# Scores of blocks 0 and 1, and of blocks 2 and 3, each in one run of 64-row products

## The reference

```
h = RMSNorm(x);  z = h @ w_in            # q, k, v of 8 heads
q, k = rope(q), rope(k)                  # two maps per head, 64 wide each
s = q @ k.T * 64**-0.5                   # per head, per map, causal
p = softmax(where(mask, s, -1e30))
a = p[map 0] - lam * p[map 1]
o = RMSNorm(a @ v) * (1 - lam_init)
```

## Time and profile before

| what | value |
|---|---|
| median of 3 runs | 1675.25 us (1673.26 to 1676.34) |
| profiled execution | span 1673.1 us, no other time is listed for it; granted TensorE clock 0.998 |
| PE busy | 1654.3 us, 99% of the span, 12028 products |
| DVE busy | 1199.4 us, 72% |
| ACT busy | 745.6 us, 45% |
| POOL busy | 139.5 us, 8% |
| DMA | 194.73 MB, mean 116 GB/s |

### The profile page before, as it was taken

One profiled execution on the slowest core, in us unless ns is written; L12 is line 12 of the kernel. 1 busy time (PEld: TensorE's weight loads), 2 busy tenths in 40 slices (PEclk: granted clock), 3 DMA queues, 4 the chain that ended last, 5 costly groups with the idle time before them and its releaser, 6 DMA issues.

```text
span 1673.1 us, 30382 instructions
## 1 busy us (share of the span) xinstructions
PE 1654.3 (99%) x12028; PEld 1598.3 (96%) x12028; DVE 1199.4 (72%) x1989; ACT 745.6 (45%) x1524; POOL 139.5 (8%) x244
## 2 busy tenths in 40 slices
PE   8999999999999999999999999999999999999997
PEld 7899999999988999999999999999999999999997
DVE  6777777777777779776444468767666786868685
ACT  5455555555555321465312344343433543544352
POOL 3222312322210000000000000000000000000001
PEclk9999999999999999999999999999999999999999
DMA  6202202202204547575221222444444833443323
GB/s 198 64 1 76 70 14 71 77 17 61 71 1 151 180 127 240 181 261 188 89 64 58 82 89 95 140 140 140 140 140 140 308 104 128 152 149 131 107 83 127
DMA packets 153071, 194.73 MB, mean 116 GB/s; under 512 B 7642, under 2 KB 121370, under 8 KB 150874
## 3 DMA queue, kind: packets, MB, share of 16 engines
q1 hardware_dynamic: 138352, 160.59, 30.0%
q10 hardware_dynamic: 14578, 32.20, 5.3%
HBM read 148.86 MB, written 44.13 MB: 115 GB/s over the span
## 4 chain that ended last, share of the span: by engine, by line
PE 95%; DVE 3%; ACT 1%; issue 1%; DMA 0%; SPq 0%; DVEq 0%; POOL 0%; ACTq 0%; POOLq 0%
PE ps L1218 36%; PE ps L948 26%; PE ps L853 16%; PE ps L912 4%; PE ps L879 3%; PE ps L902 2%; PE ps L1271 1%; PE ps L1328 1%; PE ps L883 1%; PE ps L821 1%; PE ps L846 0%; PE ps L845 0%; PE ps L863 0%; PE ps L862 0%; PE ps L1120 0%
## 5 line engine op out<-in xcount | busy, mean ns | idle before, releaser
L853 PE MATMUL ps<-w_hi,h_hi 128*128 128x384 f32 x520 | 182.0, 350 | 0.3 <-DVE w_lo L1871 0.3
L853 PE MATMUL ps<-w_hi,h_lo 128*128 128x384 f32 x520 | 176.2, 339 | 0.0
L853 PE MATMUL ps<-w_lo,h_hi 128*128 128x384 f32 x520 | 175.4, 337 | 0.0
L1218 PE MATMUL ps<-d_hi,m_hi 128*128 128x258 f32 x784 | 158.7, 284 | 0.5 <-DVE x L2537 0.4
L1218 PE MATMUL ps<-d_lo,m_hi 128*128 128x258 f32 x784 | 159.2, 284 | 0.0
L1218 PE MATMUL ps<-d_hi,m_lo 128*128 128x258 f32 x784 | 158.2, 283 | 0.0
L1408 ACT ACTIVATE prob<-ps,nbias 128x256 f32<-128x256 f32 (+7 forms) x128 | 95.0, 742 | 78.7 <-DVE nbias L1934 76.4
L1669 ACT ACTIVATE m_hi<-m_pair 128x512 fp32r<-128x512 f32 (+1 forms) x128 | 76.9, 601 | 104.1 <-PE ps L1218 90.1
L1218 PEld LDWEIGHTS ps<-d_hi,m_hi 128*128 128x128 f32 x784 | 121.6, 190 | 1.0 <-DVE x L2537 0.6
L1218 PEld LDWEIGHTS ps<-d_hi,m_lo 128*128 128x128 f32 x784 | 122.3, 190 | 0.0
L1218 PEld LDWEIGHTS ps<-d_lo,m_hi 128*128 128x128 f32 x784 | 121.9, 190 | 0.0
(11 more groups left out here) (308 smaller groups left out, 4339.4 us busy)
## 6 DMA issues: line engine op xcount, KB each, us to landing
ff_combination_scratch<-ff_st SPq DMA_DIRECT2D x14, 1806.0 KB, 6.9
d_raw<-ff_combination_scratch ACTq DMA_DIRECT2D x21, 1032.0 KB, 7.3
w_raw<-in_w_in SPq DMA_DIRECT2D x41, 512.0 KB, 5.4
kv_pages<-in_cache_k SPq DMA_DIRECT2D x32, 512.0 KB, 5.3
kv_pages<-in_cache_v SPq DMA_DIRECT2D x32, 512.0 KB, 4.5
m_pair<-in_w_up SPq DMA_DIRECT2D x16, 1024.0 KB, 9.7
m_pair<-in_w_down SPq DMA_DIRECT2D x24, 512.0 KB, 5.2
out<-kv_st SPq DMA_DIRECT2D x16, 512.0 KB
```

What stands on the lines that cost most here:

```text
L853: mm = pe.matmul(bank[0:n, 0:3 * P], a[:, kt, toks(t)], w[:, :, kt, :], start=(kt == 0 and m == 0), stop=(kt == KT - 1 and m == 2))
L1218: mm = pe.matmul(acc[:, c], w[:, kt], a[:, kt % kts, c * CW:(c + 1) * CW], start=(opens and kt == 0 and m == 0), stop=(kt == n - 1 and m = ...
```

## The change

Blocks 0 and 1: one function, `first_scores`, does the products of both and then the four masks. Block 1's scores now begin at column 128, beside those of block 0, in the same banks. Its first product no longer clears the accumulation state of the bank, since the first product of block 0 has done so. VectorE's maxima of both blocks wait for all four masks.

Blocks 2 and 3, in heads 0 to 6: `middle_scores` does the same in step 2, behind the first half of the projection of tile 2. Block 3's scores begin at column 512 (banks 3 and 5), and wait until the projection of tile 1 has been read out of bank 3. In step 3 there are no scores; the transposes of block 2's weights stand ahead of the first half of the projection of tile 3 instead of behind it. In the last head blocks 2 and 3 stay apart.

```diff
         def first_col(h, i):
-            return 512 if h == HEADS - 1 and i == 2 else 0
+            return {1: P, (2 if h == HEADS - 1 else 3): 512}.get(i, 0)
...
-            def scores(h, par, i):
...
+            def score_passes(h, par, i):
                 diag, o = i // 4, first_col(h, i)
...
-                                      k[part, par, 1, 512 * b:512 * b + n], start=(m == 0),
-                                      stop=(m == 2))
+                                      k[part, par, 1, 512 * b:512 * b + n], start=(m == 0 and i != 1),
+                                      stop=(m == 2), skip_group_check=(i < 2))
...
+            def first_scores(h, par):
+
+                pe.wait_ge(s_qklo, 8 * h + 2)
+                need(pe, s_exp, 16 * h)
+                score_passes(h, par, 0)
+                score_passes(h, par, 1)
+                causal_mask(h, 0)
+                causal_mask(h, 1)
+
+            def middle_scores(h, par):
+
+                pe.wait_ge(s_qklo, 8 * h + NTT)
+                pe.wait_ge(s_exp, 16 * h + 4)
+                score_passes(h, par, 2)
+                pe.wait_ge(s_zfree, z_before(h + 1, 2) + 1)
+                score_passes(h, par, 3)
+                causal_mask(h, 2)
+                causal_mask(h, 3)
...
                 for s in range(NTT + 1):
-                    if s < NTT:
+                    if s == 0:
+                        first_scores(h, par)
+                    elif 4 <= s < NTT:
                         scores(h, par, s)
+                    if s == 2:
+                        project(h + 1, s, 0)
+                        middle_scores(h, par)
                     if 2 <= s < NTT:
                         values(h, par, s - 2)
                     elif s == 0 and normed:
                         values(h - 1, 1 - par, NTT - 1)
-                    project(h + 1, s, 0)
+                    if s == 3:
+                        weight_transposes(h, s - 1, 0, True)
+                    if s != 2:
+                        project(h + 1, s, 0)
...
-                    if s >= 1:
+                    if s >= 1 and s != 3:
                         weight_transposes(h, s - 1, 0, True)
...
             def maximum(h, i, c):
                 n = (i + 1) * P
                 k = 16 * h + 2 * i + c + 1
-                dve.wait_ge(s_s, k)
+                dve.wait_ge(s_s, 16 * h + 4 if i < 2 else k)
```

More of the change, by code:

```diff
@@ L879, in scores, with causal_mask @@
                             pe.matmul(bank_s[:, c, o + 512 * b:o + 512 * b + n], q[part, par, 0, i * P:(i + 1) * P],
-                                      k[part, par, 1, 512 * b:512 * b + n], start=(m == 0),
-                                      stop=(m == 2))
+                                      k[part, par, 1, 512 * b:512 * b + n], start=(m == 0 and i != 1),
+                                      stop=(m == 2), skip_group_check=(i < 2))
+            def causal_mask(h, i):
+                o = first_col(h, i)
                 for c in range(2):
@@ L884, in scores @@
                               skip_group_check=True).then_inc(s_s, 1)
+            def first_scores(h, par):
[13 more added lines that the diff above has]
+                causal_mask(h, 3)
+            def scores(h, par, i):
+                if h < HEADS - 1:
+                    pe.wait_ge(s_exp, 16 * h + 2 * i)
+                    if i == 4:
+                        pe.wait_ge(s_zfree, z_before(h + 1, NTT))
+                else:
+                    if i == 2:
+                        pe.wait_ge(s_qklo, 8 * h + NTT)
+                        pe.wait_ge(s_zs, HEADS - 1)
+                    pe.wait_ge(s_exp, 16 * h + 2 * (i - 1 if i <= 3 else i))
+                score_passes(h, par, i)
+                causal_mask(h, i)
             def weight_transposes(h, i, r, proj):
@@ L1045, in last_head @@
                 for s in range(NTT + 1):
-                    if s < NTT:
+                    if s == 0:
+                        first_scores(h, par)
+                    elif 2 <= s < NTT:
                         scores(h, par, s)
```

## The result

The changed kernel takes 1680.34 us (median of 6, 1678.30 to 1681.04) against 1674.65 (median of 6, 1673.26 to 1676.34): ratio 1.0032, 95% interval 1.0021 to 1.0042, slower by 5.7 us. Forecast were 1679.4 and +4.2. The profiled execution has a span of 1678.9 and a time of 1680.87; against the 1673.1 before, the span is 5.8 longer.

What follows compares the result with a forecast made beforehand. TensorE was taken as the bound, with 95% of the span. Heads 1 to 6 at +0.52 us each (3.1), head 0 +0.72 and last head +0.4 gave +4.2 on the 1675.25 median: 1679.4 us, range 1673.5 to 1683.

Steps and rivals of the forecast that it cites:

- Part 4: Heads 0 to 6: TensorE waits 1.40 us up to projection 3 for block 2's softmax and the copy; net 1.07 later.
- T: TensorE's start on projection 2; forecast from it: maximum at 3.90 us, copy's end at 8.83, projection 3 at 8.98.
- Part 1: Scores of blocks 0 and 1 in one run: saves 0.35 us per head, 2.8 us in eight heads.
- Part 2: Scores of blocks 2 and 3 in one run, heads 0 to 6: saves 0.33 us per head, 2.3 in seven.
- Part 3: Heads 1 to 6, projection behind block 0's scores: later arrival hides the wait for weights, 0.2 us each, 1.2 in all.
- low-weights wait: Projection behind block 0's scores, heads 1 to 6: waits 1.9 us over six load-queue waits for VectorE's low half; forecast gone.
- Part 5: Last head: VectorE's first maximum waits for all four masks, so the head ends about 0.4 us later.
- Head 0: First head, which has no wait for the weights to hide: forecast 0.72 us longer.
- The first: Rival: block 2's softmax or rotation runs beside TensorE, no wait comes, the merge pays: 1669.4 us, faster; 12%.
- The second, a smaller wait: Rival: the wait is smaller or more is hidden elsewhere; net +0.2 us per head, 1676.8 us; 20%.
- The third, a second wait: Rival: transposes of previous head's output wait for ScalarE to empty their bank; six heads lose 0.4 to 0.8, 1683; 8%.

Runs made afterwards that it cites:

- e2_middle_only: Changed kernel with blocks 0 and 1 apart as before, so only blocks 2 and 3 share a run: 1682.10 us, 1.0043 against the kernel before.
- e3_masks_apart: Changed kernel with block 2's masks right behind block 2's products, ahead of block 3's: 1674.91 us, 1.0000 against the kernel before.
- e1_first_only: Changed kernel with blocks 2 and 3 as before, so only blocks 0 and 1 share a run: 1673.65 us, 0.9992 against the kernel before.
- e6_first_not_last: Kernel before with blocks 0 and 1 in one run in heads 0 to 6, the last head unchanged: 1672.28 us, 0.9985 against the kernel before.
- e4_rotation_first: Changed kernel, VectorE rotating tile 2 before block 2's weights, block 2's transposes behind projection 3's first half: 1679.71 us, 1.0026 against the kernel before.

## Why the prediction was right

The direction, the place and the mechanism were right, and the size nearly: +4.2 forecast, +4.6 in the heads, +5.7 by the runs (3.5 to 7.0 by the interval). How close the time itself came (1679.4 against 1680.34) is in part luck. It was added to the 1675.25 of three runs, and six give 1674.65. The 1.04 us by which head 0 begins later have no term in the sum. And in the heads larger errors cancel: heads 1 to 5 are 0.4 over the forecast in all, head 0 is 0.16 over, head 6 is 0.28 under.

- *Part 4, the wait.* Right in each step. The points from T on are met within 0.03 us, and e2_middle_only gives its net price alone: 1.1 per head (1.07). What made it countable is that the order on VectorE is fixed: 4.93 us from maximum to copy before the change, 4.94 after (261.60 to 266.54).
- *Part 1.* The merge of blocks 0 and 1 pays 0.30, not 0.35. After the change, from 245.69 + 0.11 to the second product of values less its 0.12 are 1.27 us for the two blocks. Before, block 0 alone took 0.75, read in the same way from the first two rows below, and block 1 alone 0.82. The mis-sized term is the price of block 1 inside the run (0.35 + 0.12): its first pair takes 0.17 and not 0.12. That is 0.05 in each of heads 0 to 6, 0.35 in all.

```profile
242.65 0.27 PE L863 MATMUL ps<-ident,kv_st 128*128 128x128 f32 x1
...
243.63 0.28 PE L912 MATMUL ps<-v_hl,aT_lo 128*128 128x256 f32 x1
...
245.39 0.34 PE L853 MATMUL ps<-w_hi,h_hi 128*128 128x384 f32 x1
```

- *Part 2.* By TensorE's rows the merge of 2 and 3 is worth 0.33 as forecast: block 2's values start their second product at 261.74 in the changed kernel, 1.83 after the end of the half projection at 259.79, against 0.99 and 1.18 for the two runs apart (block 3's read in the same way). But it could never be cashed while projection 3 waits (e3_masks_apart): it only made the wait longer. I had booked it as income and the wait in full, which gives the same sum.
- *Part 3.* The low-weights wait is gone where blocks 0 and 1 are merged and there where they are not (e1_first_only, e2_middle_only). Its worth was met too: before, 24 products took 4.41 (245.39 to 249.80); after, 36 take 6.31, so 24 take 4.21: 0.20, as forecast. In the changed kernel it pays, since the wait behind blocks 2 and 3 counts from TensorE's own mask. In head 6 this wait was 0.37 longer than in the others, and the forecast treats all six alike: that is why head 6 came out lower than forecast.
- *Part 5.* Right: 0.42 measured, 0.4 forecast, and e6_first_not_last takes it back.
- *Head 0* was 0.88 longer and not 0.72. Part 1's 0.05 is in it (e1_first_only: -0.30). The rest lies behind T: to the turned q and k of tile 3 it takes 13.20 us after the change, as counted (8.98 + 4.20), but took 12.03 before, where the counted terms give 12.11. So TensorE's own work was counted 0.08 too long for this head; which term is at fault is not shown.
- *Rivals.* The first was out by 0.6 us of chain, as argued. The second, a smaller wait, is out as well: 9.0 less TensorE's own 7.58 is the 1.4 forecast. The third, a second wait, did not occur in the changed kernel, but its margin of 0.4 was real: e4_rotation_first ran into it.

In the changed kernel, too, pairs in the same two row groups start 0.12 apart with a load each (246.45 to 246.57). The Trainium skill's rule that a load overlaps running products only where the row group differs ("TensorE: Matmul & The Clock Gate", Part 3, The mechanism) is not borne out by these rows. The same section of the Trainium skill also says that a load which targets the background weight buffer is pulled ahead of running products. With that its words and the rows agree, and the prediction, which took only the narrower sentence, was wrong to find the Trainium skill at odds with the trace. No run here shows which buffer a load went to.

## What to carry to other kernels

A saving on the engine that is busy all the time is worth what it says only up to the next signal that this engine waits for. Before work is moved, write down for each consumer behind it how long the other engines' chain is, from the instruction whose end starts it, in the kernel's own rows. As long as the order on those other engines stays, the chain's length stays (4.93 and 4.94 here), and what changes is its cover. A new order on them can change it: in e4_rotation_first the copy ended 3.96 us after the maximum's start, and what was moved behind it took 0.39 longer than in its old place. Where work is put in one run to save a switch, let what others wait for come first, or put independent work behind the run and not ahead of it: 1.04 us of products moved from one side to the other were worth 1.04 us per head here.

## What the runs showed of the hardware

Two of VectorE's operations on SBUF took longer when they ran beside GpSimd's. When e4_rotation_first put block 2's weights behind the rotation, they ran beside GpSimd's sums of the rotated tile. The seven combinations of 384 columns then took 780 ns each; in the changed kernel, with the same operands, 618. Groups by line, both kernels (busy us, mean ns):

```profile
L1985 DVE SCALAR_TENSOR_TENSOR prob<-prob,ratio 128x384 f32<-128x384 f32 x7 | 5.5, 780 | 0.2
```

```profile
L1987 DVE SCALAR_TENSOR_TENSOR prob<-prob,ratio 128x384 f32<-128x384 f32 x7 | 4.3, 618 | 0.2
```

The ratio of one column ahead of it took 0.45 us and not 0.22. VectorE and GpSimd in order of time in one head of e4_rotation_first:

```profile
263.92 0.45 DVE L1982 SCALAR_TENSOR_TENSOR ratio<-sums,nlam,rsum 128x1 f32<-128x1 f32 x1
264.40 0.78 DVE L1985 SCALAR_TENSOR_TENSOR prob<-prob,ratio 128x384 f32<-128x384 f32 x1
```

```profile
263.89 0.46 POOL L2748 TENSOR_TENSOR q_nat<-rc,rs 128x128 f32<-128x128 f32 x1 [4.49 <-DVE kv_st L1958]
264.31 0.46 POOL L2749 TENSOR_TENSOR kv_st<-rc,rs 128x128 f32<-128x128 f32 x1
```

The Trainium skill has a rule for it ("SBUF — State Buffer", SBUF: two separate sides): VectorE with two inputs in SBUF and GpSimd share a pair of ports, and the one that comes second is blocked for the whole operation of the other. The rows agree that there is a price: 0.23 us on the ratio and 0.16 on the combination. The ratio, which started behind GpSimd's first sum, ends at 264.37, and that sum at 264.35, as such a block would have it. The combination's 0.16 doesn't show a whole block, and no run tests the rule further.
